# First weight chunk second in SyncE's queue, small constants from ScalarE's queue, GpSimd's arithmetic before its fills, ScalarE's table loaded early: a hybrid decoder layer

## What is computed

```python
h = rmsnorm(x, norm_g)
proj = h @ w_in                      # 1024 -> 3072
sb_q, sb_k, sb_v, sb_gate, lru_x, lru_gate, xa_q, xa_gate = split(proj)
sb  = stick_breaking_attention(rmsnorm(q), rmsnorm(k), v)      # 8 heads x 64, strictly causal
lru = rg_lru(causal_depthwise_conv(lru_x))                     # 4 blocks x 64, gates, scan over rows
xa  = softmax_attention(rmsnorm(xq), memory keys, values)      # 4 heads x 64, 256 tokens
y = concat(sb * silu(sb_gate), lru * silu(lru_gate), xa * silu(xa_gate))
out = x + y @ w_out
```

## Time and profile before

| | us |
|---|---|
| median of 3 runs | 1522.66 |
| lowest, highest of them | 1519.68, 1522.7 |
| the profiled execution | 1522.08 |
| its span in the profile | 1520.2 |
| TensorE busy | 1481.7 (97%) |
| VectorE busy | 1044.6 (69%) |
| ScalarE busy | 930.4 (61%) |
| GpSimd busy | 304.4 (20%) |

### The profile page before, as it was taken

The page is one execution under the profiler, slowest core; times in us unless marked ns, Lnnn a source line. Parts: engine busy times, 40 slices in busy tenths (PEclk is TensorE's granted clock), DMA queues, the critical chain, the costliest instruction groups (busy, mean ns, idle before and its releaser), DMA issues.

```text
span 1520.2 us, 31129 instructions
## 1 busy us (share of the span) xinstructions
PE 1481.7 (97%) x11404; PEld 720.1 (47%) x11404; DVE 1044.6 (69%) x1908; ACT 930.4 (61%) x1720; POOL 304.4 (20%) x305
## 2 busy tenths in 40 slices
PE   4999999999999999999999999999999999999997
PEld 2444444444444444444444444444444444444443
DVE  6988766676666676666676666667666667666684
ACT  6888655676555676555576555576555577555582
POOL 3132211222211222111222111222111222111220
PEclk9999999999999999999999999999999999999999
DMA  9455746655645655555654554665554665554655
GB/s 360 188 151 108 161 107 137 139 124 120 143 109 126 147 121 120 137 117 118 152 122 117 135 124 110 152 126 119 127 130 109 148 133 119 121 140 106 143 112 140
DMA packets 468041, 205.83 MB, mean 135 GB/s; under 512 B 440800, under 2 KB 441248, under 8 KB 466848
## 3 DMA queue, kind: packets, MB, share of 16 engines
q1 hardware_dynamic: 467712, 205.16, 57.5%
q10 hardware_dynamic: 288, 0.13, 0.0%
HBM read 55.53 MB, written 50.53 MB: 70 GB/s over the span
## 4 chain that ended last, share of the span: by engine, by line
PE 92%; DVE 4%; DMA 1%; ACT 1%; issue 1%; SPq 0%; ACTq 0%; DVEq 0%
PE bank L1965 28%; PE bank L1966 27%; PE bank L1967 27%; PE bank L2176 2%; PE bank L2012 2%; PE bank L2036 1%; DVE w_pair L1329 1%; PE bank L2063 1%; PE bank L2054 1%; DMA wo_pair<-in_w_in 1%; PE bank L2107 1%; PE bank L2102 0%; PE bank L2104 0%; PE bank L2103 0%; PE bank L1949 0%
## 5 line engine op out<-in xcount | busy, mean ns | idle before, releaser
L1965 PE MATMUL bank<-w_pair,x_hi 128*128 128x512 f16 x1520 | 577.7, 380 | 4.8 <-DVE w_pair L1329 4.8
L1966 PE MATMUL bank<-w_pair,x_hi 128*128 128x512 f16 x1520 | 576.8, 380 | 0.0
L1967 PE MATMUL bank<-w_pair,x_lo 128*128 128x512 f16 x1520 | 576.8, 379 | 0.0
L1055 ACT ACTIVATE qk_raw<-bank,unscale 128x512 f32<-128x512 f32 x32 | 22.0, 687 | 428.4 <-PE bank L1967 424.4
L1965 PEld LDWEIGHTS bank<-w_pair,x_hi 128*128 128x128 f16 x1520 | 148.7, 98 | 182.4 <-issue 9.8
L1967 PEld LDWEIGHTS bank<-w_pair,x_lo 128*128 128x128 f16 x1520 | 148.9, 98 | 180.0 <-issue 1.1
L1966 PEld LDWEIGHTS bank<-w_pair,x_hi 128*128 128x128 f16 x1520 | 148.9, 98 | 168.6 <-issue 1.8
L1965 PE MATMUL bank<-wo_pair,y_hi 128*128 128x512 f16 x480 | 181.9, 379 | 0.0
L1966 PE MATMUL bank<-wo_pair,y_hi 128*128 128x512 f16 x480 | 181.9, 379 | 0.0
L1967 PE MATMUL bank<-wo_pair,y_lo 128*128 128x512 f16 x480 | 181.9, 379 | 0.0
L798 POOL TENSOR_TENSOR fail_and_take<-fail_and_take,seen 128x512 f32<-128x512 f32 x32 | 40.7, 1272 | 677.4 <-ACT fail_and_take L958 677.4
(11 more groups left out here) (280 smaller groups left out, 2428.0 us busy)
## 6 DMA issues: line engine op xcount, KB each, us to landing
xy<-in_x SPq DMA_DIRECT2D x32, 512.0 KB, 3.8
spare<-in_x SPq DMA_DIRECT2D x30, 512.0 KB, 3.9
out<-spare SPq DMA_DIRECT2D x29, 512.0 KB, 2.6
gate_kept<-gate SPq DMA_DIRECT2D x32, 256.0 KB, 2.3
v_kept<-v_sb SPq DMA_DIRECT2D x32, 256.0 KB, 2.1
fail_and_take<-v_sb SPq DMA_DIRECT2D x64, 128.0 KB, 2.3
q_kept<-heads_t SPq DMA_DIRECT2D x32, 256.0 KB, 3.9
k_kept<-heads_t SPq DMA_DIRECT2D x32, 256.0 KB, 4.1
```

Source lines behind the costliest of these rows:

```text
L1965: pe.matmul(dst, hi[:, k, :], pair[:, 0, k, :], start=k == 0, stop=False)
L1966: pe.matmul(dst, hi[:, k, :], pair[:, 1, k, :], start=False, stop=False)
L1967: last = pe.matmul(dst, lo[:, k, :], pair[:, 0, k, :], start=False, stop=k == KD - 1)
```

## The change

SyncE's queue loses the two loads of constants, so that the first chunk is its second transfer. ScalarE's queue gets them: the table of constants ahead of everything, the gain rows behind the identity's write. Behind these ScalarE runs a Square on one column, in a new slice `squares_ready` that nobody reads, for which the compiler places the table load there. On GpSimd the fill of 0.5 and its multiplication come first, with a wait between them, and the fills of ones, masks and border follow. The tile `columns` grows from 64 to 66 columns.

```diff
@@ -92,7 +92,7 @@
 
 
 
-        columns = sb("columns", [P, 64])
+        columns = sb("columns", [P, 66])
         taken = [0]
 
         def few(n):
@@ -209,6 +209,7 @@
         left_max = few(1)
         left_all = few(1)
         go_on = sb("go_on", [P, 1], I32)
+        squares_ready = few(1)
         mx = few(HX)
         neg_mx = few(HX)
         den = few(HX)
@@ -499,8 +500,6 @@
                 sp.dma_start(staged_out(7, slice(6, KD)), w_out_g[1][:, 6:KD, :]).then_inc(stage_loaded[3], 16)
 
             sp.dma_start(xy[:, :], x_t[0]).then_inc(x_loaded, 16)
-            sp.dma_start(given[:, :], per_partition).then_inc(const_loaded, 16)
-            sp.dma_start(gate[:, 0, 0:4 * HD], gain_rows).then_inc(const_loaded, 16)
             load_chunk(0)
             sp.dma_start(x_t32[:, :, :], x_turned[0]).then_inc(xt_loaded, 16)
             sp.wait_ge(stage_loaded[STAGE[0]], 16)
@@ -727,13 +726,13 @@
 
         @block.gpsimd
         def _(pool):
+            pool.memset(mhalf_c[:, :], 0.5).then_inc(zeroed, 1)
+            pool.wait_ge(zeroed, 1)
+            pool.tensor_scalar(mhalf_c[:, :], mhalf_c[:, :], -1.0, None, ALU.mult).then_inc(zeroed, 1)
             pool.memset(ones[:, :], 1.0).then_inc(ones_made, 1)
-            pool.memset(mhalf_c[:, :], 0.5).then_inc(zeroed, 1)
             pool.memset(seen[:, :], 1.0)
             pool.memset(restart[:, :], 0.0).then_inc(zeroed, 1)
             pool.memset(conv_in[:, :, :], 0.0).then_inc(zeroed, 1)
-            pool.wait_ge(zeroed, 3)
-            pool.tensor_scalar(mhalf_c[:, :], mhalf_c[:, :], -1.0, None, ALU.mult).then_inc(zeroed, 1)
             pool.wait_ge(zeroed, 4)
 
             def band_masks():
@@ -1223,8 +1222,11 @@
                 if after:
                     mix_high(1)
 
+            act.dma_start(given[:, :], per_partition).then_inc(const_loaded, 16)
             act.wait_ge(ident_rows_made, 2)
             act.dma_start(ident_flat, ident_rows).then_inc(ident_moved, 16)
+            act.dma_start(gate[:, 0, 0:4 * HD], gain_rows).then_inc(const_loaded, 16)
+            act.activation(squares_ready, ident_rows[:, 0:1], ACT.Square)
             act.wait_ge(ident_moved, 16)
             flat = ident_flat.rearrange("r c -> (r c)")[0:P * P].rearrange("(p j) -> p j", j=P)
             act.dma_start(ident[:, :], flat).then_inc(ident_moved, 16)
```

## The result

The changed kernel took 1526.43 us (median of 8 runs, 1525.54 to 1526.81), the kernel before in the same comparison 1522.54 (8 runs, 1519.68 to 1523.88): a ratio of 1.0028, with a 95% interval of 1.0018 to 1.0037. The change makes the kernel 3.9 us slower. The forecast was 1523.2 with a range of 1520.3 to 1527.0. The range holds the result because its upper end was drawn to take in most of rival 2 (1527.1); the likeliest case doesn't hold. A time within 0.2% of before had the chance 0.72, and the measured one went past that bound.

What follows compares the result with a forecast made beforehand. TensorE, busy 97% of the span, was taken as the bound, so only its start could move. VectorE's 1.4 us delay less 0.29 slack gave +1.1 on the profiled 1522.08: 1523.2 us, range 1520.3 to 1527.0.

Steps and rivals of the forecast that it cites:

- rival 2: At the start, identity's write served behind the whole chunk, landing near 12; scaling 5.3 us late, 1527.1 us; chance 0.20.
- the likeliest case: At the start, late gain rows put VectorE's diagonal near 15.6, scaling of x near 16.8; total 1523.2 us; chance 0.58.
- What bounds the kernel: TensorE is busy 97% of the span; the change can only move the start of its full stretch, through the first 60 us.
- Part 1, the chunk: SyncE's queue: first chunk, issued second, lands 0.56 us earlier, at 11.4; bounds 0 and 0.94 us.
- Part 2, the gain rows: ScalarE's queue: gain rows land at 12.0 instead of 6.2, making VectorE's scaling of x 1.4 us later, at 16.8.
- Part 2, the identity's write: ScalarE's queue: write still issued at 1.22 to 1.25 and served before the chunk is done; read back issued before 8.
- Part 3, GpSimd: GpSimd's start: first arithmetic 0.89 us earlier after a fixed wait, fills moved behind it; row factor still near 13.8, price zero.
- Part 4, the table and the columns: ScalarE's start: 1.28 us table load moves from 6.14 to about 2.1, inside a wait; two more columns; both priced zero.
- Rival 1: At the start, identity's write and gain rows arrive before the chunk's packets, gain rows near 6; 1521.5 us; chance 0.18.
- Rival 3: At the start, GpSimd's 12.57 limits and the queue effects cancel: 1522.1 us; no separate chance, inside the forecast's own case.
- rival 4: Tile addresses behind the added columns move and affect transfers or TensorE's reads over 1400 us, 2.8 us either way; chance 0.04.
- The sum: Whole kernel: VectorE's 1.4 us delay at 15.44, less 0.29 slack at 59.89, moves everything from 60 us by +1.1.

Runs made afterwards that it cites:

- the experiment on the order in ScalarE's queue: The changed kernel with the identity's write first on ScalarE's queue and the small table second; 1523.29 us, ratio 1.0006 to the kernel before.
- everything early: Changed kernel with table and gain rows as one load heading ScalarE's queue, identity made on-chip by VectorE and GpSimd, GpSimd's other fills after the row factor; 1521.53 us.

## Why the prediction failed where it did

**What bounds the kernel: right.** The whole difference arose in the first 20 us, came through at 60 us less a few tenths (+4.06 at the scaling, +3.91 at line 1300) and stayed at +3.92 until 1490.76.

**Part 1, the chunk: right in kind, too small.** I took 0.56 us and bounded it by the 0.94 of issue. The chunk was there by 9.89, 2.07 us before. In the five traces without the gain rows ahead of it the chunk's landing stands at 9.69 to 10.28, in the three with them at 11.13, 11.61 and 11.96. The order costs the chunk more than the 0.33 us that their bytes take, and more than the 0.94 us that I gave as the bound; through what, no run here singles out. On the result it had no effect, because VectorE's side decided.

**Part 2, the gain rows: right.** Forecast 12.0, measured 11.72; the experiment on the order in ScalarE's queue shows the path that follows from it, with the scaling at 17.16 (forecast 16.8).

**Part 2, the identity's write: the step that failed.** The forecast's likeliest case needs the write to be served early, and against rival 2 it said: "packet-by-packet alternation, which lets 8 small packets through before the chunk is done". The alternation is real: 137 packets of the write against 133 of SyncE's queue from 4 to 9 us. The conclusion from it was wrong, and the text held the numbers to see it: the chunk has 8 packets per engine as well. Eight small packets, each behind one large packet, are through when the eighth large one is. Alternation by packet shares the turns, not the time, so the small load lands with the large one: the write at 10.06, the chunk by 9.89. For the gain rows the prediction reckoned just so ("alternate with the chunk's 8", and land with it or after it); for the write, which stood nearer to the chunk, it did not. The sign it named, a read back issued before 8, failed at 10.08. Rival 2 came near the result (diagonal at 19.5 forecast, 18.27 measured; scaling 20.7 and 19.50; 1527.1 and 1526.43), but for another reason: it had the write served behind the whole chunk. Its shift was 5.0 us against 3.9 measured; the times agree better than that because all forecasts started from the one profiled execution, 1522.08, and not from the median. Its point of decision, a landing of the write of about 9 us on, fits (10.06 decides, 5.6 doesn't), but no run lies between. Chance 0.20 was too low for a case that both orders, the block of packets and the alternation, lead to.
The Trainium skill, "DMA: Bandwidth & Descriptors", section "Queues, rings and completion order", has an engine drain a packet of some 9 to 17 descriptors from one ring before it turns to the next. The trace differs from a reading in which a load's pieces on an engine are one such unit: it has 28 and 28, 26 and 25 records in two windows of 1 us. Here the measurement decides; for this load both readings come to a landing with the chunk or behind it.

**Part 3, GpSimd: right here, not in general.** The first arithmetic came at 11.55 (0.89 earlier was forecast, 1.02 it was), and the row factor ended at 13.73 (forecast 13.8). Price zero, under cover. But the wait on which this rested, taken as fixed, isn't; see below.

**Part 4, the table and the columns: right.** The table load stands at 2.21; with everything but the queue moves in place the ratio is 1.0000. Rival 1 fell: the gain rows landed late (11.72). Rival 3 fell with the result, and rival 4 with the run that has everything but the queue moves: whatever the wider tile does lies within that run's interval.

**The sum.** +1.1 was made of +1.4 at the scaling less 0.29. With the write in the tie it is +4.06 less 0.15 (63.80 - 59.89 = 3.91). Without the tie, in the experiment on the order in ScalarE's queue, it is 1.72 at the scaling, from which the sum would make 1.43, and 0.81 at the end: the 0.29 at 59.89 isn't all the slack that VectorE has. The time of that kernel, 1523.29 against the forecast's 1523.2, agrees in part by luck, since its median lies 0.55 above the kernel before and the forecast's shift was 1.1.

## What to carry to other kernels

When a small load may share the transfer engines with a large one from another queue, count packets per engine on both sides, not bytes. In these traces a load second in ScalarE's queue landed with the chunk whenever the chunk was second in SyncE's: the identity's write (64.5 KB, 8.8 us), the gain rows (128 KB, 9.0) and even the table of constants (18 KB, 9.0). With the gain rows beside it the write took 4.4 us, and every load at the head of ScalarE's queue 3.5 to 4.6. Whatever is chained behind the late one starts there, and a detour of two chained loads met a chunk twice (8.8 and 8.1 us). Before a load is moved out of the way of another, look which third load then stands beside it.

## What was unexpected

**GpSimd's start.** Its first arithmetic instruction follows an idle time whose end the profile puts down to "issue" (once, with the queue moves alone, to the end of ScalarE's squares). Over eight kernels this is 10.73, 10.66, 11.62, 8.15, 11.21, 10.58, 9.56 and 9.61 us. Four of them have the same program on GpSimd, the changed kernel (10.66), the two with another order or place of one load (11.21 and 10.58) and the one with both loads back on SyncE (8.15), so it depends on what goes on elsewhere or scatters from one execution to the next; with one trace of each this stays open. The Trainium skill, "GPSIMD Engine Reference", section "Instruction dispatch", names about 6 us without a visible instruction for the first call to a freshly loaded kernel; the waits here are longer, and no run shows whether they are of that kind.

**The clock near the end.** Spans and steady shifts don't agree to the microsecond. From VectorE's line 1298 for the sixth chunk (59.89 in the earlier trace rows) to the marker at 1486.84 all eight traces take 1426.6 to 1427.1 us, so up to there the shift holds to half a microsecond. From the marker to the end it is 32.2 to 35.1 us. Most of this lies in the last 48 products, and first in 32 of them; these are their rows and one window each over the last 18 us (window, us, busy time of PE, PEld, DVE, ACT and POOL, then the granted clock, DMA share, GB/s). First the kernel before:

```profile
1502.73 8.41 PE L2063 MATMUL bank<-wo_pair,turned 128*128 128x512 f16 x32 [3.43 <-DMA turned<-spare]
```

```profile
1502.00:1520.00 18.00, 11.86 (x48) 4.96 (x48) 1.72 (x7) 0.00 (x0) 0.38 (x1) 0.88 0.48 133
```

The kernel with the identity on GpSimd, whose window begins within the 32 products:

```profile
1501.74 9.84 PE L2065 MATMUL bank<-wo_pair,turned 128*128 128x512 f16 x32 [3.38 <-DMA turned<-spare]
```

```profile
1503.00:1521.00 18.00, 12.04 (x46) 4.89 (x44) 1.65 (x6) 0.00 (x0) 0.00 (x0) 0.78 0.35 112
```

The kernel with everything early:

```profile
1500.28 7.08 PE L2067 MATMUL bank<-wo_pair,turned 128*128 128x512 f16 x32 [3.39 <-DMA turned<-spare]
```

```profile
1498.00:1516.00 18.00, 10.53 (x48) 4.62 (x48) 3.31 (x10) 0.00 (x0) 0.38 (x1) 1.00 0.57 148
```

For the same 48 products TensorE was busy 11.86 us at a mean granted clock of 0.88, and 10.53 us at 1.00: a stretch at the lower level (1.2 of 2.4 GHz) cost 1.33 us, all of it in the first 32 products (8.41 against 7.08). In the second kernel it was longer (0.78; 9.84 us), 1.43 us more than before, which is most of why a kernel 0.92 us ahead at 1486 us ends 0.8 us behind. TensorE had stood idle for 3.4 us ahead of these products in all three, so the idle time alone doesn't tell them apart. Of the 3.6 us by which the last kernel's span is shorter than before (1516.6 against 1520.2), 2.46 are the steady shift, and the other 1.1 are about this stretch's size; the median of its runs gained only 1.33 us. For a change at the front that is worth a microsecond, the steady shift inside the kernel is thus the sharper measure of one execution, and the runs' medians say how much of it can be told from scatter.
